# Seven block products in place of eight in one turn of each of seven groups of 1024 columns of the second block's input projection

## The chip, the cores and the metric

The kernel runs on one core of a Trainium2 chip. The metric is the device time of one execution in microseconds (us), the median of the runs. Engines are named as in the profile: PE is TensorE (matmuls), DVE is VectorE, ACT is ScalarE, POOL is GpSimd, SP is SyncE, which issues most DMAs.

## The reference, cut to what matters

```python
# first block, kind 0: gated MLP over 256 tokens, D_MODEL 2048, D_INNER 4096
h = rmsnorm(x, a_norm); z = h @ w_in; ...; x = x + (y * silu(gate)) @ w_out; x = rmsnorm(x, final_norm)
# second block
h = rmsnorm_2(x, norm1_g)
z = h @ w_in                                  # 2048 x 10256
fq, fk = rmsnorm_2 over each head of z        # 8 heads of 128
fv = z[..., 2048:3072]
a_out = forgetting_attention(fq, fk, fv, log_sigmoid(z_f + bias))
mq, mk, mv, m_o = z[..., 4 heads of 128, 128, 256, 256]
m_out = rmsnorm_2(mlstm_chunkwise(mq, mk, mv, i, log_f)) * sigmoid(m_o)
merged = sigmoid(g_a) * (a_out @ w_proj_a) + sigmoid(g_m) * (m_out @ w_proj_m)
x = x + merged @ w_out
h2 = rmsnorm_2(x, norm2_g); u = causal_dwconv(h2 @ w_up); x = x + (silu(u_gate) * u_val) @ w_down
```

All of it is float32, for 256 tokens.

## The kernel before

**Tiling.** Weights stream from HBM in chunks of 256 rows by 512 columns (128 x 1024 in SBUF, 512 KB). SP loads them into a ring of four (`RING`). Every chunk is split in two: ACT rounds it to `w_hi` (L1101), DVE subtracts that from the chunk and gives `w_lo` (L1551). A product in full precision is then three matmuls of 512 columns, hi by hi, hi by lo and lo by hi. A chunk costs PE 12 matmuls: 2 row blocks, 2 token halves, 3 each.

**Order.** All engines walk one list, `ITEMS`. `split(phase, k)` on ACT and on DVE works four items ahead: it waits until PE has done item k, whose ring place comes free, and makes `w_hi` and `w_lo` of item k+4. The steps of ACT and DVE that belong to slot `c` of a phase stand in program order behind that split. PE waits for `lo_ready` before each item.

**Seven products.** In some phases a group has 1024 columns (four PSUM banks of `g`), and in some of its turns of four chunks the 2 x 2 block product is made with seven block products (Strassen-Winograd) of 6 matmuls each in place of four chunks of 12. That takes sums of activations (`sums_of_rows`, `sums_high`, `sums_low`), sums of weight blocks, and sums of the products 1, 5, 6 and 7, which stand in banks of `xs` of their own. In phases `v`, `out1`, `gm0`, `gm1`, `out2` and `down` DVE makes four sums of weight blocks for each such turn (`block_sums`, L1556). In phase `ug` one turn of each of eight groups is made so, with one block sum on DVE and three by adding transfers that POOL issues (`add_block`, L2228). There DVE adds the own products in four instructions (L1751 to L1757) and the halves of the result in two (L1764, L1770).

**Phases around the change.** `vv` (values, 32 chunks, four groups of 512 columns) and `side` (96 chunks: four groups q and k of the attention heads, q and k of the m heads, two groups of output gates, four of gates a) run as plain chunks on PE line L633. Each group has one of two halves of `g`, and ACT takes it out of PSUM. `side` is followed by `gm0`, whose first item is a product; its sums of activations are made by DVE in `side` at slots 88 and 91 (`SUMS_AT` -8, -5; L1641 to L1647), its blocks at the splits of slots 92 on.

Each of the first four groups of `side` passes through `z`: ACT copies it out (slot 8n+7), ACT squares it (slot 8n+8), DVE reduces and makes the mean square (slot 8n+9, L1945 to L1950), POOL makes the power -1/2 (L2213), DVE makes the factor and scales `z` (slot 8n+10, L1956 and L1959), PE turns `z` (`qk_turned`, L681, slots 13, 21, 29, 37), ACT copies to `qk`. The 12 heads start at slot 22 and take four slots each: at step 0 PE makes the scores of head n and the values of head n-1 and DVE the row maximum, at step 1 ACT makes the exponential and DVE the probabilities, at step 3 PE turns them.

## Time and profile before

| | us |
|---|---|
| median of 3 runs | 2088.88 |
| lowest, highest | 2088.44, 2089.41 |
| the profiled execution | 2088.49 |
| its span | 2086.6 |
| PE busy in it | 2079.8 |
| DVE busy | 1575.4 |
| ACT busy | 1142.5 |
| POOL busy | 37.6 |

Busy time is a share of the whole span and says nothing of a stage. `vv` runs from 704 to 794 us and `side` from there to 1098 us. PE's busy time counts each matmul from issue to end, some 390 ns, while the next one starts about 227 ns after it; a short gap of PE doesn't show as idle, and distances of starts tell more.

### The profile page before, as it was taken

The numbers are of one execution on the slowest core, as the hardware profiler recorded it, in microseconds if no ns is written. First come the engines' busy times: TensorE is split into PE (matmuls) and PEld (weight loads), VectorE is DVE, ScalarE is ACT, GpSimd is POOL, SyncE is SP. The second block draws the span as 40 slices with busy tenths as digits, with TensorE's granted clock in tenths as the row PEclk, the third lists the DMA queues.
The fourth block names the chain that finished last, engine by engine and source line by source line (L and its number), as shares of the span: only waits on it lengthen the run. The fifth ranks groups of instructions, "written<-read, shape, count | busy, mean of one in ns | idle before, by whom it ended". The sixth has DMA issues, their size and how long they took to land.

```text
span 2086.6 us, 25362 instructions
## 1 busy us (share of the span) xinstructions
PE 2079.8 (100%) x9952; PEld 1741.3 (83%) x9952; DVE 1575.4 (75%) x1774; ACT 1142.5 (55%) x1354; POOL 37.6 (2%) x41
## 2 busy tenths in 40 slices
PE   9999999999999999999999999999999999999999
PEld 8888888888888887888888888888888888888887
DVE  7988888887888654655669668867777777779986
ACT  6766555555556544554455455555555555555553
POOL 0000000000000000000000000000000000000000
PEclk9999999999999999999999999999999999999999
DMA  9667777778764655544464656455565565556763
GB/s 338 211 197 216 227 235 220 214 245 237 260 229 142 208 192 168 168 159 162 150 219 167 220 172 217 156 188 186 182 194 190 182 199 185 181 183 234 224 206 132
DMA packets 115559, 417.00 MB, mean 200 GB/s; under 512 B 12912, under 2 KB 13680, under 8 KB 114800
## 3 DMA queue, kind: packets, MB, share of 16 engines
q1 hardware_dynamic: 109440, 394.66, 56.4%
q0 software_dynamic: 3456, 12.58, 3.4%
q10 hardware_dynamic: 2544, 8.14, 1.2%
q8 instruction: 79, 1.29, 0.3%
q14 instruction: 40, 0.33, 0.0%
HBM read 413.23 MB, written 2.10 MB: 199 GB/s over the span
## 4 chain that ended last, share of the span: by engine, by line
PE 94%; DVE 3%; DMA 1%; ACT 1%; issue 1%; ACTq 0%; DVEq 0%
PE g L736 34%; PE g L633 21%; PE xs L658 8%; PE g L658 8%; PE xs L759 7%; PE g L763 5%; PE xs L662 4%; PE g L662 4%; DVE w_lo L1551 1%; PE xs L681 1%; DMA gz_block<-in_stream 1%; ACT w_hi L1101 1%; PE xs L918 0%; PE xs L798 0%; DMA raw<-in_stream 0%
## 5 line engine op out<-in xcount | busy, mean ns | idle before, releaser
L1551 DVE TENSOR_TENSOR w_lo<-raw,w_hi 128x1024 fp32r<-128x1024 f32 x643 | 783.0, 1223 | 394.8 <-ACT w_hi L1101 386.9
L1101 ACT ACTIVATE w_hi<-raw 128x1024 fp32r<-128x1024 f32 x643 | 679.6, 1058 | 615.4 <-PE g L633 222.3
L736 PE MATMUL g<-w_hi,in_both 128*128 128x512 f32 x1120 | 356.7, 390 | 1.3 <-DVE w_lo L1622 0.4
L633 PE MATMUL g<-w_hi,mid_both 128*128 128x512 f32 x1024 | 326.6, 394 | 0.0
L736 PEld LDWEIGHTS g<-w_hi,in_both 128*128 128x128 f32 x1120 | 210.2, 188 | 47.0 <-issue 1.8
L633 PEld LDWEIGHTS g<-w_hi,mid_both 128*128 128x128 f32 x1024 | 192.3, 188 | 39.6
L736 PE MATMUL g<-w_lo,in_both 128*128 128x512 f32 x560 | 217.9, 389 | 0.0
L633 PE MATMUL g<-w_lo,mid_both 128*128 128x512 f32 x512 | 199.4, 389 | 0.0
L658 PE MATMUL g<-mlp_both,w_hi 128*128 128x512 f32 x704 | 176.8, 393 | 0.0
L658 PE MATMUL xs<-mlp_both,w_hi 128*128 128x512 f32 x704 | 176.3, 392 | 0.0
L658 PEld LDWEIGHTS g<-mlp_both,w_hi 128*128 128x128 f32 x704 | 126.5, 189 | 22.8
L658 PEld LDWEIGHTS xs<-mlp_both,w_hi 128*128 128x128 f32 x704 | 126.6, 189 | 22.6
L736 PEld LDWEIGHTS g<-w_lo,in_both 128*128 128x128 f32 x560 | 105.1, 188 | 21.3
L633 PEld LDWEIGHTS g<-w_lo,mid_both 128*128 128x128 f32 x512 | 96.3, 188 | 19.1
L662 PEld LDWEIGHTS g<-mlp_both,w_lo 128*128 128x128 f32 x704 | 96.2, 190 | 7.0
L662 PEld LDWEIGHTS xs<-mlp_both,w_lo 128*128 128x128 f32 x704 | 96.1, 190 | 6.8
L662 PE MATMUL g<-mlp_both,w_lo 128*128 128x256 f32 x704 | 98.3, 282 | 0.0
L662 PE MATMUL xs<-mlp_both,w_lo 128*128 128x256 f32 x704 | 98.2, 282 | 0.0
L736 PE MATMUL g<-w_hi,f_hi 128*128 128x512 f32 x240 | 93.6, 390 | 0.1
L736 PE MATMUL g<-w_lo,f_hi 128*128 128x512 f32 x240 | 93.4, 389 | 0.0
L736 PE MATMUL g<-w_hi,f_lo 128*128 128x512 f32 x240 | 93.4, 389 | 0.0
L1101 ACT ACTIVATE w_hi<-d_block 128x1024 fp32r<-128x1024 f32 x49 | 52.0, 1062 | 56.8 <-PE g L736 39.1
(440 smaller groups left out, 3182.6 us busy)
## 6 DMA issues: line engine op xcount, KB each, us to landing
raw<-in_stream SPq DMA_DIRECT2D x643, 512.0 KB, 3.8
d_block<-in_stream SPq DMA_DIRECT2D x28, 512.0 KB, 4.6
o_block<-in_stream SPq DMA_DIRECT2D x24, 512.0 KB, 4.4
v_block<-in_stream SPq DMA_DIRECT2D x20, 512.0 KB, 3.9
ge_block<-in_stream POOLq DMA_DIRECT2D x15, 512.0 KB, 5.5
gm_block<-in_stream SPq DMA_DIRECT2D x12, 512.0 KB, 4.9
ge_block<-in_stream SPq DMA_DIRECT2D x10, 512.0 KB, 4.7
gl_block<-in_stream POOLq DMA_DIRECT2D x6, 512.0 KB, 6.2
```

The lines of the kernel that those rows point to most:

```text
L633: ins = mm(G[buf][:, t, :], a[:, kt, at_t], w[:, slot, j * COLS:(j + 1) * COLS], start=(kt == 0 and n == 0), stop=(last and j == ROWS_PER_ ...
L658: mm(UP[buf][:, b, :, :], w_hi[:, slot, j * COLS + b * P:j * COLS + (b + 1) * P], a_both[:, :, kt, :], start=(kt == 0), stop=False, skip_g ...
L662: ins = mm(UP[buf][:, b, 0, :], w_lo[:, slot, j * COLS + b * P:j * COLS + (b + 1) * P], a_both[:, 0, kt, :], start=False, stop=(last and j ...
L681: ins = turn(TR[:, b, t * P:(t + 1) * P], of[:, t, b * P:(b + 1) * P], ident[:])
L736: ins = mm(GG[:, bank, :], a[:, kt, t * P:(t + 1) * P], w[:, slot, half_chunk(j)], start=n == 0 and opens(item, bank), stop=ended and n == ...
L759: ins = mm(XS[:, own[p], :], a, w[:, slot, half_chunk(j)], start=first and opens_own(item), stop=last and j == 1 and n == 2, skip_group_ch ...
L763: ins = mm(GG[:, RESULT_OF[p], :], a, w[:, slot, half_chunk(j)], start=first and opens(item, RESULT_OF[p]), stop=False, skip_group_check=True)
L1101: activation(w_hi[:, n % RING, :], of[:], ACT.Copy).then_inc(hi_ready, 1)
L1551: v.tensor_tensor(w_lo[:, n % RING, :], of, w_hi[:, n % RING, :].bitcast(F32), ALU.subtract).then_inc(lo_ready, 1)
```

## The change

Phases `vv` and `side` become wide phases: groups of 1024 columns, two in `vv` and six in `side`. In all but the fourth group of `side` turn 0 is made by seven products, in the manner of `ug`. Such a group has 19 items in place of 16 chunks. Three of the 19 (places 5, 10 and 14) have no slot, so that the slots `c` and the steps that go by them stay 16 to a group. ACT copies products 1, 5 and 7 out of their banks; DVE adds them from SBUF, then adds each half of the result in SBUF (`half`). ACT no longer takes these groups from PSUM. The q and k tiles are squared at slots 14, 16, 30 and 32, and turned three slots later; the m heads' q and k at 47 and 49. The mean square and the scaling stay one and two slots behind the squares. The sums of activations for turn 0 are made at the seventh last item of `out1`. POOL's powers are moved to the places of its queue where their inputs come.

```diff
--- before.py
+++ after.py
@@ -67,9 +67,9 @@
 HEAD_AT = 22
 ALL_HEADS = HEADS + M_HEADS
-QK_T_AT = (13, 21, 29, 37, 43, 51)
+QK_T_AT = (17, 19, 33, 35, 47, 49)
+Q_SQUARES_AT = (14, 16, 30, 32)
 QK_TILE = (0, 8, 4, 12, 16, 20)
-VV_OUT = (10, 15, 23, 31)
...
+SUM_TURNS = {"v": (3, 2), "out1": (4, 5), "vv": (0,), "down": (0, 1, 2, 6), "gm0": (3, 2), "out2": (1,)}
+SUMS_AT = {"v": (4, 8), "out1": (2, 6), "vv": (-7,), "down": (3, 6, 9, 64), "gm0": (-8, -5), "out2": (-7,)}
...
-WIDE = tuple(WIDE_STEPS) + ("ug",)
...
+MID_TURN = 0
+MID_PAIRED = ((1, "C0"), (1, "C1"), (1, "C2"), (1, "C3"), (2, "C0"), 1, 5, (2, "C1"), (2, "C2"), (2, "C3"), 7, 6,
+              (3, "C0"), (3, "C1"), 3, 2, 4, (3, "C2"), (3, "C3"))
+MID_SINGLE = ((1, "C0"), (1, "C1"), (1, "C2"), (1, "C3"), (2, "C0"), 1, (2, "C1"), 5, (2, "C2"), (2, "C3"), 7,
+              (3, "C0"), 6, (3, "C1"), 3, 2, 4, (3, "C2"), (3, "C3"))
+MID_PLAIN = tuple((_t, f"C{2 * _h + _k}") for _h in range(2) for _t in range(4) for _k in range(2))
+MID_ORDER = {"vv": (MID_PAIRED,) * 2,
+             "side": (MID_PAIRED, MID_SINGLE, MID_SINGLE, MID_PLAIN, MID_SINGLE, MID_SINGLE)}
+MID_HALF_ENDS = (16, 18)
+NO_SLOT = (5, 10, 14)
+SLOTS = {}
+for _name, _orders in MID_ORDER.items():
+    SLOTS[_name] = []
+    for _g, _order in enumerate(_orders):
+        _c = 16 * _g
+        for _k in range(len(_order)):
+            if len(_order) > 16 and _k in NO_SLOT:
+                SLOTS[_name].append(None)
+            else:
+                SLOTS[_name].append(_c)
+                _c += 1
+SPREAD = ("ug", "vv", "side")
+WIDE = tuple(WIDE_STEPS) + SPREAD
...
+TWO_BANKS = {1: 0, 5: 1, 7: 0, 6: 1}
+ONE_BANK = {1: 1, 5: 1, 7: 1, 6: 1}
...
+BLOCKS_AT = {FIRST_ITEM["vv"] - 5: ("vv", B11), FIRST_ITEM["vv"] - 4: ("vv", B12),
+             FIRST_ITEM["side"] - 3: ("side", B12), FIRST_ITEM["side"] - 2: ("side", B11),
+             FIRST_ITEM["side"] + 66: ("side", B11, 4), FIRST_ITEM["side"] + 67: ("side", B12, 4),
+             FIRST_ITEM["side"] + 88: ("side", B11, 5), FIRST_ITEM["side"] + 89: ("side", B12, 5),
...
+            def opens_mid(item):
+                phase, g, p = item.phase, item.group, item.product
+                ahead, copied, bank = own_ahead(phase, g), 2 * mid_quads(phase, g), own_banks(phase, g)
+                if p == 1:
+                    pe.wait_ge(sem["own_read"], ahead)
+                    if phase == "side" and g in (1, 2):
+                        pe.wait_ge(sem["qk_ready"], 2 * g)
+                    if phase == "side" and g == 4:
+                        pe.wait_ge(sem["scores_read"], ALL_HEADS)
+                if p in (7, 6) and (phase, g) == ("vv", 0):
+                    pe.wait_ge(sem["g_lo_ready"], 4)
+                before = [k for k in (1, 5, 7, 6) if bank[k] == bank[p]]
+                before = before[before.index(p) - 1] if before.index(p) else None
+                if before == 1:
+                    pe.wait_ge(sem["p1_ready"], ahead + 1)
+                if before == 5:
+                    pe.wait_ge(sem["own_copied"], copied + 1)
+                if before == 7:
+                    pe.wait_ge(sem["own_copied"], copied + 2)
...
+            for n in range(items_of("vv")):
+                c = SLOTS["vv"][n]
+                at_item = FIRST_ITEM["vv"] + n
+                item = ITEMS[at_item]
+                pe.wait_ge(lo_ready, at_item + 1)
+                if not item.product and item.group == 0:
+                    pe.wait_ge(sem["g_lo_ready"], item.turn + 1)
+                if item.product == 5 and item.group == 0:
+                    pe.wait_ge(sem["sums_lo_ready"], sums_ahead("vv") + 1)
+                step = wide_product if item.product else wide_chunk
+                step(item, norm_mid.hi, norm_mid.lo, at_item % RING).then_inc(mm_done, 1)
...
                 if n < 4:
                     pe.wait_ge(sem["q_scaled"], n + 1)
                 else:
-                    buf, _, read = group_of("side", n)
-                    pe.wait_ge(group_read[buf], read)
+                    pe.wait_ge(sem["m_scaled"], n - 3)
+                pe.wait_ge(sem["own_read"], own_ahead("side", n // 2 + 1))
                 if n:
                     pe.wait_ge(sem["qk_ready"], n)
                 if heads_before(QK_T_AT[n] + 1):
                     pe.wait_ge(sem["scores_read"], heads_before(QK_T_AT[n] + 1))
-                blocks_turned(z).then_inc(sem["qk_turned"], 1)
+                blocks_turned(wide("side", n // 2).half[n % 2]).then_inc(sem["qk_turned"], 1)
...
-            for c in range(96):
-                one("side", c // 8, c % 8, tokens("side", c // 8, norm_mid.hi, norm_mid.lo))
+            for n in range(items_of("side")):
+                c = SLOTS["side"][n]
+                at_item = FIRST_ITEM["side"] + n
+                item = ITEMS[at_item]
+                pe.wait_ge(lo_ready, at_item + 1)
+                step = wide_product if item.product else wide_chunk
+                step(item, norm_mid.hi, norm_mid.lo, at_item % RING).then_inc(mm_done, 1)
+                if c is None:
+                    continue
...
+            def mid_copies(at_item):
...
+                item = ITEMS[at_item]
+                phase, g, p = item.phase, item.group, item.product
+                if p not in (1, 5, 7):
+                    return
+                if p in (1, 5) and (phase, g) in (("vv", 1), ("side", 0)):
+                    act.wait_ge(sem["vv_out"], (1 if p == 1 else 2) + (2 if phase == "side" else 0))
+                if p == 1 and (phase, g) == ("side", 5):
+                    act.wait_ge(sem["m_values_read"], M_HEADS)
+                act.wait_ge(mm_done, at_item + 1)
+                to = {1: wide(phase, g).p1, 5: wide(phase, g).p5, 7: wide(phase, g).p7}[p]
+                activation(to, XS[:, own_banks(phase, g)[p], :], ACT.Copy).then_inc(sem["p1_ready" if p == 1 else "own_copied"], 1)
+            def half_result(phase, n):
+                buf, _, read = group_of(phase, n)
+                act.wait_ge(group_read[buf], read)
+                return wide(phase, n // 2).half[n % 2]
...
+            def vv_out(n):
+                if n == 0:
+                    act.wait_ge(sem["scale_ready"], 2)
+                by_token(vv[:, :, col_block(n)], half_result("vv", n), ACT.Copy, scale).then_inc(sem["vv_out"], 1)
+            def gate_a_tanh(n):
+                by_token(ga[:, GA_PLACE[n - 8]], half_result("side", n), ACT.Tanh, scale_half).then_inc(sem["ga_ready"], 1)
...
-            for c in range(96):
-                split("side", c)
+                if c in (14, 16, 30):
+                    vv_out((14, 16, 30).index(c))
+            for n in range(items_of("side")):
+                c = SLOTS["side"][n]
+                split("side", n)
+                mid_copies(FIRST_ITEM["side"] + n)
+                if c is None:
+                    continue
                 sums_high("gm0", c - 96)
+                if c == 0:
+                    vv_out(3)
...
-                if c % 8 == 7:
+                if c in (55, 63):
                     n = c // 8
                     product, read, _ = done("side", n)
...
-                if c % 8 == 0 and 8 <= c <= 32:
-                    n = c // 8 - 1
-                    buf, _, read = group_of("side", n)
-                    act.wait_ge(group_read[buf], read)
+                    by_token(mo[:, :, col_block(n - 6)], product, ACT.Tanh, scale_half).then_inc(read, 1)
+                if c in (46, 48):
+                    half = half_result("side", c // 2 - 19)
+                    by_token(half, half, ACT.Copy, scale).then_inc(sem["m_scaled"], 1)
+                if c in (78, 80, 94):
+                    gate_a_tanh({78: 8, 80: 9, 94: 10}[c])
+                if c in Q_SQUARES_AT:
+                    n = Q_SQUARES_AT.index(c)
                     if n:
                         act.wait_ge(sem["q_ms_ready"], n)
-                    activation(z_sq[:], z[:], ACT.Square).then_inc(sem["z_sq_ready"], 1)
+                    activation(z_sq[:], half_result("side", n)[:], ACT.Square).then_inc(sem["z_sq_ready"], 1)
...
+                sums_low("vv", n - items_of("out1"))
+                sums_of_rows("vv", n - items_of("out1"), norm_mid.hi, norm_mid.lo)
...
+            def mid_own_products(phase, n):
...
+                for name, g in GROUPS_BY_PRODUCTS:
+                    if name != phase:
+                        continue
+                    of, at_6 = wide(phase, g), product_item(phase, g, MID_TURN, 6)
+                    after = n - at_6
+                    if after == 0:
+                        dve.wait_ge(sem["p1_ready"], own_ahead(phase, g) + 1)
+                        dve.wait_ge(mm_done, at_6 + 1)
+                        link(v.tensor_tensor(of.u_a, of.p1, XS[:, own_banks(phase, g)[6], :], ALU.subtract))
+                    if after == 1:
+                        dve.wait_ge(sem["own_copied"], 2 * mid_quads(phase, g) + 2)
+                        link(v.tensor_tensor(of.p7, of.p7, of.u_a, ALU.add))
+                    if after == 2:
+                        link(v.tensor_tensor(of.u_a, of.p5, of.u_a, ALU.add))
+                    if after == 3:
+                        v.tensor_tensor(of.p5, of.p5, of.p7, ALU.add).then_inc(sem["own_read"], 1)
...
+            def mid_results(phase, n):
+                for name, g in GROUPS_BY_PRODUCTS:
+                    for h in range(2):
+                        if name == phase and n == half_end(phase, g, h):
+                            buf, end, _ = group_of(phase, 2 * g + h)
+                            half = wide(phase, g).half[h]
+                            dve.wait_ge(mm_done, end)
+                            dve.wait_ge(sem["own_read"], own_ahead(phase, g) + 1)
+                            v.tensor_tensor(half[:], G[h], half[:], ALU.subtract if h else ALU.add).then_inc(group_read[h], 1)
...
-            for c in range(96):
-                split("side", c)
+            for n in range(items_of("side")):
+                c = SLOTS["side"][n]
+                mid_results("side", FIRST_ITEM["side"] + n)
+                split("side", n)
+                mid_own_products("side", FIRST_ITEM["side"] + n)
+                if c is None:
+                    continue
...
-                if c % 8 == 1 and 9 <= c <= 33:
-                    n = c // 8 - 1
+                if c - 1 in Q_SQUARES_AT:
+                    n = Q_SQUARES_AT.index(c - 1)
...
-                if c % 8 == 2 and 10 <= c <= 34:
-                    n = c // 8 - 1
+                if c - 2 in Q_SQUARES_AT:
+                    n = Q_SQUARES_AT.index(c - 2)
                     dve.wait_ge(sem["q_rstd_ready"], n + 1)
+                    if n:
+                        dve.wait_ge(sem["q_scaled"], n)
...
-                    by_head = z[:].rearrange("p t (h d) -> p (t h) d", d=P)
+                    by_head = wide("side", n // 2).half[n % 2][:].rearrange("p t (h d) -> p (t h) d", d=P)
...
                 item = ITEMS[n]
-                if item.phase != "ug" or item.product not in (1, 5, 6):
+                if item.phase not in SPREAD or item.product not in (1, 5, 6):
                     return
-                q, g = quad_of(item), item.group
+                q = quad_of(item)
                 product, to, b = {1: (7, B12, B22), 5: (6, B11, B22), 6: (4, B11, B21)}[item.product]
                 if item.product == 1:
                     pool.wait_ge(sem["block_sums"], sums_made(q, 5))
                 else:
                     pool.wait_ge(lo_ready, n + 1)
-                p.dma_start(wide("ug", g).blocks[to][:], stream[block_row(q, b)], accum_op=ALU.add).then_inc(
+                p.dma_start(wide(item.phase, item.group).blocks[to][:], stream[block_row(q, b)], accum_op=ALU.add).then_inc(
                     sem[f"block_added{product}"], 16)
...
-                if n == FIRST_ITEM["vv"]:
+                if n == FIRST_ITEM["vv"] + 13:
                     rstd(n_rstd[:, 0:2], n_ms[:, 0:2], "ms_ready", 2, "rstd_ready")
                     rstd(n_rstd[:, 2:4], n_ms[:, 2:4], "ms_ready", 3, "rstd_ready")
-                if n == FIRST_ITEM["side"]:
-                    for k in range(4):
+                for k in range(4):
+                    if n == item_at_slot("side", Q_SQUARES_AT[k] + 1) + RING:
                         rstd(q_rstd[:], q_ms[:], "q_ms_ready", k + 1, "q_rstd_ready")
-                    for m in range(M_HEADS):
+                for m in range(M_HEADS):
+                    if n == item_at_slot("side", HEAD_AT + 4 * (HEADS + 1 + m)) + RING:
                         rstd(m_rstd[:], m_ms[:], "m_ms_ready", m + 1, "m_rstd_ready")
```

## Rows read from the trace of the kernel before

**Rows 1.** The page, part 1: busy time of each engine.
```profile
PE 2079.8 (100%) x9952; PEld 1741.3 (83%) x9952; DVE 1575.4 (75%) x1774; ACT 1142.5 (55%) x1354; POOL 37.6 (2%) x41
```
**Rows 2.** Stretches `ug`, `vv`, `side` and start of `gm0`: busy us (instructions), clock, DMA.
```profile
core 0: us, PE busy (x) PEld busy (x) DVE busy (x) ACT busy (x) POOL busy (x), PEclk, DMA share, GB/s
200.00:500.00 300.00, 300.00 (x1353) 248.98 (x1352) 243.94 (x237) 169.07 (x188) 16.12 (x19) 1.00 0.75 229
704.00:794.00 90.00, 90.00 (x407) 74.70 (x406) 48.31 (x53) 45.89 (x63) 1.41 (x2) 1.00 0.59 192
794.00:1098.00 304.00, 303.64 (x1395) 245.99 (x1394) 177.11 (x325) 155.38 (x221) 12.05 (x8) 1.00 0.51 170
1098.00:1113.00 15.00, 15.00 (x68) 12.42 (x67) 14.62 (x13) 9.54 (x10) 0.00 (x0) 1.00 0.53 178
```
**Rows 3.** Timeline of PE: start, length, engine, line: a chunk, product 5 and product 7 begin.
```profile
1099.88 0.39 PE L736 MATMUL g<-w_hi,mid_both 128*128 128x512 f32 x1
...
1102.60 0.39 PE L759 MATMUL xs<-w_hi,gm_sums_hi 128*128 128x512 f32 x1
...
1103.96 0.39 PE L759 MATMUL xs<-w_hi,gm_sums_hi 128*128 128x512 f32 x1
```
**Rows 4.** Timeline of all engines, slots 9 to 13 of `side`: one q tile.
```profile
828.43 1.23 DVE L1551 TENSOR_TENSOR w_lo<-raw,w_hi 128x1024 fp32r<-128x1024 f32 x1 [1.53 <-ACT w_hi L1101]
...
829.58 1.21 DVE L1945 TENSOR_REDUCE q_ss<-z_sq 128x8 f32<-128x1024 f32 x1
...
831.47 2.54 POOL L2213 TENSOR_TENSOR q_rstd<-q_ms,minus_half 128x8 f32<-128x8 f32 x1 [97.16 <-DVE q_ms L1950]
...
834.44 1.22 DVE L1959 TENSOR_TENSOR z<-z,q_factor 128x1024 f32<-128x1024 f32 x1
...
837.97 1.03 PE L681 MATMUL xs<-ident,z 128*128 128x128 f32 x8
838.22 1.06 ACT L1101 ACTIVATE w_hi<-raw 128x1024 fp32r<-128x1024 f32 x1 [1.66 <-PE g L633]
838.76 0.48 PE L633 MATMUL g<-w_hi,mid_both 128*128 128x512 f32 x1
```
**Rows 5.** Timeline of POOL: the power of the fourth q tile.
```profile
905.27 1.64 POOL L2213 TENSOR_TENSOR q_rstd<-q_ms,minus_half 128x8 f32<-128x8 f32 x1 [24.07 <-DVE q_ms L1950]
```
**Rows 6.** Timeline of PE at step 0 of a head: scores and values.
```profile
876.82 0.44 PE L915 MATMUL xs<-head_row,ones_r 64*128 64x384 f32 x1
...
878.38 0.39 PE L943 MATMUL xs<-probs_t,vv 128*128 128x128 f32 x2
```
**Rows 7.** Timeline of DVE: last slots of `side`, first items of `gm0`.
```profile
1088.99 1.23 DVE L1551 TENSOR_TENSOR w_lo<-raw,w_hi 128x1024 fp32r<-128x1024 f32 x1 [1.50 <-ACT w_hi L1101]
1090.14 1.22 DVE L1596 TENSOR_TENSOR gm_sums_lo<-gm_sums,gm_sums_hi 128x1024 fp32r<-128x1024 f32 x1
1091.27 1.22 DVE L1641 TENSOR_TENSOR gm_rows<-mid_both 128x1024 f32<-128x1024 f32 x1
...
1094.12 1.22 DVE L1551 TENSOR_TENSOR w_lo<-gm_block,w_hi 128x1024 fp32r<-128x1024 f32 x1
1095.47 1.23 DVE L1556 TENSOR_TENSOR gm_block<-gm_block,gm_block 128x1024 f32<-128x1024 f32 x1
...
1102.42 1.22 DVE L1551 TENSOR_TENSOR w_lo<-gm_block,w_hi 128x1024 fp32r<-128x1024 f32 x1
```
**Rows 8.** Timeline of DVE in `ug`: an own-product sum and the instruction behind it, a half's result.
```profile
257.66 0.68 DVE L1755 TENSOR_TENSOR ge_gate<-xs,ge_gate 128x512 f32<-128x512 f32 x1
258.38 1.23 DVE L1551 TENSOR_TENSOR w_lo<-raw,w_hi 128x1024 fp32r<-128x1024 f32 x1
...
261.26 1.22 DVE L1764 TENSOR_TENSOR ge_act<-g,ge_act 128x1024 f32<-128x1024 f32 x1
```
**Rows 9.** What reads or writes `ge_block` in `ug`: issue, and time to landing of its DMAs.
```profile
L2228 POOL DMA_DIRECT2D ge_block<-in_stream x15: 865/865/1056, 179.2 to 378.9; - x15
...
DMA to landing us min/median/max: 4.2/5.4/7.5
```

127 lines of the change are left out of this document (83 added, 44 removed).

## Prediction

> **What bounds the kernel now.** I read the page's busy times first [rows 1]: PE has work in flight in all but 7 us of the span, DVE in 75%, ACT in 55%. That is a mean, so the table by stage comes next [rows 2]: in `vv` PE is in flight 90.00 us of 90 and in `side` 303.64 of 304, at granted clock 1.00 (2.4 GHz), while DVE has 48 and 177 us of work. The stage behind them is another matter: from 1098 to 1113 DVE works 14.62 us of 15. Then the distances of starts: a chunk of 12 matmuls takes 2.72 us, from 1099.88 to 1102.60, and a product of six takes 1.36, from there to 1103.96 [rows 3]. So 0.227 us a matmul is the price on the path in both stages, and whatever makes PE wait for DVE is added to it.
>
> Last the time that a step needs, counted from the end of a PE item, E. PE turns the first q tile at 837.97 [rows 4]; four chunks earlier, at 827.09, slot 9 ended. DVE's `w_lo` starts 1.34 after E (828.43), and its next instruction at 829.58.
>
> **What is taken away.** Seven groups (two in `vv`, five in `side`) each make eight blocks as seven: 48 matmuls become 42. 7 x 6 x 0.2267 = 9.5 us less on PE, all of it on the path.
>
> **What is added, beside other work.** For each group: three more items to split (DVE 3 x 1.14, ACT 3 x 1.06), one block sum (1.15), four own-product sums of 0.72 and two results of 1.14 [rows 7, 8], 9.7 us of DVE in 40. The stage's DVE share goes from 54% and 58% to about 78% and 76%. `ug` carries the same scheme with 243.94 of 300 us of DVE and 0.75 of the DMAs, and PE is in flight in all of it [rows 2]. So the means leave room, and the scheme alone I cost at nothing: PE and the ring of four cover it. ACT's three copies of products (0.6 each, an estimate at half of a full 1.06 tile) have cover in both stages at 51% ACT. The three added DMAs of a group land in 4.2 to 7.5 us [rows 9]; product 4 in the order with lone products is the tightest. Its block can be asked for 2.6 us after place 8 ends, lands 0.9 + 5.4 later and needs 2.3 for the split, 11.2 in all, where PE comes to it after 13.6: nothing, and nothing up to a landing of 7.8. The moved sums at the end of `out1` put 4 us of DVE on one item of 2.72 and plain chunks follow: 0 to 1 us, taken as 0, since the items behind have 1.6 us each to spare. In POOL's queue each power now stands behind the adding transfers whose inputs come before it, and a transfer takes POOL 0.87 us [rows 9], ahead of the power's start: nothing. The removed ACT copies out of PSUM were off the path: nothing.
>
> **What comes onto the path, first place: the q and k tiles.** Before, a tile's mean square is made at slot 9, scaled at 10, turned at 13: PE has four chunks, 10.9 us, between the end of slot 9 and the turn, and DVE finishes at 834.44 + 1.22 = 835.66, 8.6 after it [rows 4]. So 2.3 us are spare. After, the mean square is made at slot 15, scaled at 16, and turned at 17: two chunks, 5.4 us. The chain doesn't get shorter. From the start of the reduction to the end of the scaling it takes 835.66 - 829.58 = 6.08 us, of which POOL's power is 2.54 [rows 4].
> - First tile. At slot 15 DVE first adds the second half (starts at E + 0.3, 1.14), then splits (1.14): the reduction starts at E + 2.6, the scaling ends at E + 8.7, PE is there at E + 5.4. Wait 3.2.
> - Second tile, turned at slot 19. Its reduction stands on DVE behind the first scaling, a split and the block sum for product 1: 1.14 + 1.25 + 6.08 = 8.5 after that scaling. PE has the first turn (0.9, rows 4 from 837.97 to 838.76) and slots 18 and 19: 6.4. Wait 2.1.
> - Third tile, turned at 33, as the first, with a head's step 0 and 1 on DVE ahead of it and in POOL's shadow: 3.3.
> - Fourth tile, at 35: PE has two steps more, a turn of probabilities and the scores and values at slot 34, 1.95 us [rows 6], which nearly cover it: 0 to 0.5, taken as 0.3.
>
> Together 8.9 us. If POOL's power takes 1.64 us, as once [rows 5], the four come to about 5.9. I take 8.9, since the other rows of that instruction are 2.54. Behind these waits are PE's next items, whose splits are done by then, so they cost nothing more and give nothing back.
>
> **Second place: the seam of `side` and `gm0`.** Before, DVE makes the second sums of activations (1091.27 to 1094.12) and then, without a pause, the splits and block sums of `gm0`; the split of its product 7 ends at 1102.42 + 1.22 = 1103.64 [rows 7] and PE wants it at 1103.96 [rows 3]. Only 0.3 us are spare. After, the sums stay at slots 88 and 91, now places 9 and 13 of a group of 19 items whose tail has product 6, then 3, 2 and 4, and DVE's own-product sums. Take time 0 at PE's end of place 12. Place 13 ends at 2.72 and DVE starts its split 1.34 later, at 4.06. In order it then has, up to the split of `gm0`'s product 7: three splits (3.4), three splits with block sums (7.2, like 1094.12 to 1096.62 three times less the waits), two `sums_low` (2.26), the sums of activations (2.85), three own-product sums (2.16) and two results (2.28). That is 20.1 and ends at 24.2. PE's items until then are 3 chunks (places 13, 17, 18), 3 products, and `gm0`'s product 1, chunk, product 5: 4 x 2.72 + 5 x 1.36 = 17.7. Wait 6.5 in all, seen in parts: at place 18 (its split is behind the sums), at product 1 of `gm0` (own bank not yet read), at its first chunk and at product 7. It can be 5.5 if a link wait or two falls away. It can be 7.4 if the block of product 4 lands at the slow end of 7.5 [rows 9]. Behind product 7, DVE catches up within three items. I add nothing.
>
> **Sum.** 2088.49 - 9.5 + 8.9 + 6.5 = 2094.4 for an execution like the profiled one. That one lay 0.39 under the median of 2088.88, so the forecast in medians is 2094.8. A measurement of this kernel can tell about 0.2% (4.2 us) from no change, so the bounds are 2084.7 and 2093.1.
>
> **Rivals.**
> - *The change works as in `ug`, with no waits.* For it: the same scheme in rows 2, at more DVE load. Against it: `ug` has no POOL step ahead of a turn two slots later and no sums of activations in its tails. Time 2088.9 - 9.5 = 2079.4. This is the other side, and one mechanism decides it: whether DVE is ahead of PE at the two places. It needs the q chain under 5.4 us from the end of slot 15, where rows 4 has 8.6. Chance 0.08.
> - *Only one place is real.* PE's waits at the tiles give the ring time, or the seam's DVE work is overlapped more than in my order: -9.5 + 8.9 gives 2088.3, -9.5 + 6.5 gives 2085.9. Chance 0.15, time 2088.
> - *The product tails under heads are too dense.* In groups 1, 2 and 4 of `side` DVE has a head's steps beside own-product sums; probabilities of the head of place 12 are ready some 0.2 us before PE turns them after place 16. If that chain is 1 us longer, three groups give 3 us: 2097.8. Chance 0.12.
> - *The clock falls in the waits.* In the trace PE never waits 3 us and its clock is 1.00 in each stretch [rows 2], so no row shows what follows a wait of 3.2. At 1.2 GHz a chunk would take 2.72 us more at most; one after each of two long waits gives 2094.8 + 5.4 = 2100.2. Chance 0.08. The Trainium skill (TensorE: Matmul & The Clock Gate, "HAM oscillation") says that PE's clock is halved after idle time in the middle of a kernel. By that rule the long waits would be followed by slow matmuls; no run here shows it yet.
>
> **How the numbers follow.** The forecast has 0.57, with its own range 2090.8 (short powers and the lean seam, 5.9 + 5.5) to 2096.5. Range: 2086.0 takes in most of the one-place case and leaves the no-wait case out; 2100.0 takes in dense tails and most of the clock's. Slower by over 0.2%: all of the dense and clock cases, and four fifths of the forecast's, 0.66. Faster: the no-wait case and a little of the seam-only one, 0.10. The same: 0.24.
>
> **What would show it.** Right: PE's start distances in `vv` stay at 0.227 us with 42 matmuls fewer in both stages; PE waits of 2 to 3.5 us just before the turns of q and k, at three of four, with POOL's power ending 1.6 us before each; DVE without a pause from slot 91 to `gm0`'s product 7, and PE waiting for `w_lo` and `own_read` there. Wrong: a turn with no wait, DVE idle at the seam, or a wait in `vv` or at product 4. The prediction fails most likely by the size of the tile waits, which rest on POOL's 2.54.

## The result, and the profile after

The changed kernel takes 2100.45 us (median, 2098.47 to 2101.49), the kernel before beside it 2088.74: 1.0055 times as long, 95% interval 1.0037 to 1.0072. The direction was as forecast, the time 5.7 us above the forecast and 0.45 above the range. Measured again later on another occasion it took 2098.69. The profiled execution took 2100.55 us, its span is 2098.8.

The page's busy time of PE (time, share of the span, instructions) has the 42 matmuls fewer, and yet PE works less of the span:

```profile
PE 2076.6 (99%) x9910; PEld 1735.3 (83%) x9910; DVE 1644.8 (78%) x1850; ACT 1171.6 (56%) x1393; POOL 55.5 (3%) x62
```

By stage (busy time and instructions per engine, granted clock of PE, DMA share), against [rows 2]:

```profile
core 0: us, PE busy (x) PEld busy (x) DVE busy (x) ACT busy (x) POOL busy (x), PEclk, DMA share, GB/s
704.00:795.00 91.00, 91.00 (x411) 75.53 (x410) 69.08 (x75) 56.31 (x77) 7.69 (x8) 1.00 0.78 234
...
845.00:870.00 25.00, 18.91 (x82) 15.10 (x80) 14.84 (x23) 10.02 (x10) 6.06 (x4) 0.86 0.52 135
870.00:1098.00 228.00, 225.61 (x1036) 182.43 (x1036) 166.19 (x297) 130.46 (x196) 15.07 (x16) 1.00 0.62 187
1098.00:1111.00 13.00, 9.77 (x41) 7.14 (x40) 12.59 (x16) 7.35 (x8) 0.00 (x0) 1.00 0.57 213
1111.00:1122.00 11.00, 8.47 (x31) 6.51 (x30) 9.61 (x9) 5.63 (x7) 0.00 (x0) 0.84 0.44 146
```

In `vv` PE is in flight all the time at full clock, as before. It is missing 6.1 us from 845 to 870, 2.4 from there to 1098, 3.2 from 1098 to 1111 and 2.5 behind that. In two of the stretches the granted clock is 0.86 and 0.84, where each stretch before had 1.00. What PE waited for from 795 to 1120 (total, times, the longest):

```profile
engine line waited for: us in total, times, longest us
PE xs L781 <- DVE mq_half L2177: 6.1, 2, 4.8
PE xs L884 <- DVE w_lo L1725: 2.5, 1, 2.5
PE xs L781 <- DVE mk_half L2177: 2.4, 1, 2.4
...
PE xs L1017 <- DVE gl L2137: 0.8, 1, 0.8
```

These are the two places of the prediction: line 781 turns a q or k tile and waits for the scaling, and the rest of the large ones belong to the seam. Line 1017, the running sums of the gates, was in no step.

**The tiles.** All engines around the first two turns (start, length, engine, line, operation; in brackets the idle time before it and its releaser):

```profile
844.97 1.21 DVE L2161 TENSOR_REDUCE q_ss<-z_sq 128x8 f32<-128x1024 f32 x1
...
845.94 0.39 PE L861 MATMUL g<-w_hi,mid_both 128*128 128x512 f32 x1
...
846.70 1.22 DVE L1725 TENSOR_TENSOR w_lo<-raw,w_hi 128x1024 fp32r<-128x1024 f32 x1
...
846.87 2.57 POOL L2431 TENSOR_TENSOR q_rstd<-q_ms,minus_half 128x8 f32<-128x8 f32 x1 [27.82 <-DVE q_ms L2166]
...
851.15 1.97 PE L781 MATMUL xs<-ident,mq_half 128*128 128x128 f32 x8 [4.83 <-DVE mq_half L2177]
...
852.77 0.78 PE L861 MATMUL g<-w_hi,mid_both 128*128 128x512 f32 x1
...
853.77 1.05 PE L861 MATMUL g<-w_hi,mid_both 128*128 128x512 f32 x2
...
855.41 1.66 POOL L2431 TENSOR_TENSOR q_rstd<-q_ms,minus_half 128x8 f32<-128x8 f32 x1 [0.62 <-DVE q_ms L2166]
...
855.79 0.62 PE L861 MATMUL g<-w_hi,mid_both 128*128 128x512 f32 x2
...
858.06 1.23 DVE L1725 TENSOR_TENSOR w_lo<-raw,w_hi 128x1024 fp32r<-128x1024 f32 x1 [2.74 <-ACT w_hi L1243]
...
859.21 0.39 PE L861 MATMUL g<-w_hi,mid_both 128*128 128x512 f32 x1
...
860.87 0.86 PEld L781 LDWEIGHTS xs<-ident,mq_half 128*128 128x128 f32 x8 [1.69 <-DVE mq_half L2177]
```

The last matmul before the first turn begins at 845.94, the turn at 851.15, 5.21 later where a matmul takes 0.227: 4.99 us of waiting. Before the second turn it is 860.87 - 859.21 - 0.23 = 1.43. The chunk at 852.77 starts at half clock: it has a matmul of 0.78 and at 853.77 two in 1.05; at 855.79 two take 0.62 again. The granted clock was 0.5 for 6.8 us, from 848.3, still within the wait, to 855.1. The third tile:

```profile
903.57 1.66 POOL L2431 TENSOR_TENSOR q_rstd<-q_ms,minus_half 128x8 f32<-128x8 f32 x1 [25.86 <-DVE q_ms L2166]
...
904.16 0.39 PE L861 MATMUL g<-w_hi,mid_both 128*128 128x512 f32 x1
...
906.94 0.86 PEld L781 LDWEIGHTS xs<-ident,mk_half 128*128 128x128 f32 x8 [2.81 <-DVE mk_half L2177]
```

906.94 - 904.16 - 0.23 = 2.55. The fourth turn has no wait. POOL's power took 2.57 us for the first tile and 1.66 for the others. The first starts 0.17 us behind the start of a split on DVE (846.70); the second, at 855.41, starts with no split running, DVE's next being at 858.06.

**The seam.** PE around product 7 of `gm0`, and what DVE has in that time:

```profile
1111.34 0.39 PE L884 MATMUL xs<-w_hi,gm_sums_lo 128*128 128x512 f32 x1
1114.27 0.60 PE L884 MATMUL xs<-w_hi,gm_sums_hi 128*128 128x512 f32 x1 [2.53 <-DVE w_lo L1725]
1114.66 0.63 PE L884 MATMUL xs<-w_lo,gm_sums_hi 128*128 128x512 f32 x1
```

```profile
1111.86 1.22 DVE L2083 TENSOR_TENSOR mb_half<-g,mb_half 128x1024 f32<-128x1024 f32 x1
1113.00 1.22 DVE L1725 TENSOR_TENSOR w_lo<-gm_block,w_hi 128x1024 fp32r<-128x1024 f32 x1
```

DVE goes from instruction to instruction and ends the split at 1114.22; PE starts product 7 at 1114.27 and had been free since 1111.57: 2.70 us. Then come matmuls of 0.63 in place of 0.39, for 3.4 us at granted clock 0.5. The same difference of starts gives 1.75 at place 18, 1.06 at product 1 and 0.91 at the first chunk of `gm0`: 6.42 with product 7.

### The profile page after: what moved, and what is told of

The parts are those of the page before. It is cut to its first block, busy times and chain, and to the rows that moved or that the text cites. A ratio compares the mean times of both kernels' runs of the same rounds, so it can differ in the third digit from the quotient of the medians.

```text
span 2098.8 us, 25523 instructions
## 1 busy us (share of the span) xinstructions
PE 2076.6 (99%) x9910; PEld 1735.3 (83%) x9910; DVE 1644.8 (78%) x1850; ACT 1171.6 (56%) x1393; POOL 55.5 (3%) x62
## 4 chain that ended last, share of the span: by engine, by line
PE 89%; DVE 6%; DMA 2%; ACT 2%; issue 1%; POOL 0%; ACTq 0%; DVEq 0%
PE g L861 44%; PE xs L884 9%; PE xs L758 8%; PE g L758 8%; PE g L888 5%; PE g L733 4%; PE xs L762 4%; PE g L762 4%; DVE w_lo L1725 2%; ACT w_hi L1243 1%; PE xs L781 1%; DMA raw<-in_stream 1%; DMA gz_block<-in_stream 1%; PE xs L923 0%; PE xs L1053 0%
## 5 line engine op out<-in xcount | busy, mean ns | idle before, releaser
L1725 DVE TENSOR_TENSOR w_lo<-raw,w_hi 128x1024 fp32r<-128x1024 f32 x629 | 765.2, 1223 | 312.2 <-ACT w_hi L1243 303.4
L1243 ACT ACTIVATE w_hi<-raw 128x1024 fp32r<-128x1024 f32 x629 | 664.4, 1058 | 550.4 <-PE g L861 233.8
L861 PE MATMUL g<-w_hi,mid_both 128*128 128x512 f32 x960 | 312.8, 395 | 2.3 <-DVE w_lo L1725 2.3
L861 PEld LDWEIGHTS g<-w_hi,mid_both 128*128 128x128 f32 x960 | 181.3, 189 | 40.7 <-DVE w_lo L1725 3.2
L861 PE MATMUL g<-w_lo,mid_both 128*128 128x512 f32 x480 | 187.7, 391 | 0.0
L861 PEld LDWEIGHTS g<-w_lo,mid_both 128*128 128x128 f32 x480 | 90.7, 189 | 18.1
```

The source lines that it names most:

```text
L861: ins = mm(GG[:, bank, :], a[:, kt, t * P:(t + 1) * P], w[:, slot, half_chunk(j)], start=n == 0 and opens(item, bank), stop=ended and n == ...
L1243: activation(w_hi[:, n % RING, :], of[:], ACT.Copy).then_inc(hi_ready, 1)
L1725: v.tensor_tensor(w_lo[:, n % RING, :], of, w_hi[:, n % RING, :].bitcast(F32), ALU.subtract).then_inc(lo_ready, 1)
```

## The experiments

"Waits" below are distances of starts less the 0.227 of a matmul, as above. Every time is the median beside that of the kernel before on the same chip, which was 2088.87 to 2088.99 in all of them. Only one execution of a kernel has a trace. Of the others the record has the time, the span and the mean granted clock; a stretch of 3.4 us at half clock lowers that mean by 0.0008, from 1.000 to 0.999. It was 1.000 in all but one of 68 executions of the kernel before, and 0.997 to 0.998 in the four of the changed kernel.

### Which places hold the loss

**no_scaling** takes the chain out of the q and k tiles (squares on ACT, mean square and scaling on DVE, power on POOL) and leaves the turns where they are. The result lacks the norm of q and k.

```diff
-                    pe.wait_ge(sem["q_scaled"], n + 1)
+                    buf, _, read = group_of("side", n)
+                    pe.wait_ge(group_read[buf], read)
...
-                if c in Q_SQUARES_AT:
...
-                if c - 1 in Q_SQUARES_AT:
...
-                if c - 2 in Q_SQUARES_AT:
...
-                        rstd(q_rstd[:], q_ms[:], "q_ms_ready", k + 1, "q_rstd_ready")
```


> The changed kernel with the norm of q and k left out (squares, mean square, power and scaling; the tiles are turned as soon as the halves are added), so a part of the computation is missing. Theory A (PE waits at the turns because the chain of DVE, POOL and DVE from the mean square to the scaling is longer than the two chunks that PE has): all waits at the turns vanish, 9.0 us, and the 6.8 us at half clock behind the first of them too, worth about 2; time 2100.45 - 11 = 2089.5, with the four waits at the seam to gm0 unchanged at 6.4 us. Theory B (PE waits in these stages because DVE as a whole is too full in a group of 19 items): half or less of the waits goes, since the DVE work left out is only 13 us, and waits appear elsewhere; 2095 or more.

2089.54 (1.0002, interval 0.9993 to 1.0012). In the trace no wait at a turn is left, and no stretch at half clock; the waits of the seam are the same to 0.02 us (1.75, 1.06, 0.91, 2.72). From the first matmul of `vv` to the first of `pa0`, the phase behind `gm0`, this trace has 434.1 us, the changed kernel's 447.1 and the one before 435.4. So the tile waits (9.0) and the two stretches at half clock (3.7, below) make up nearly all of the 12.9 between the two. The stretch at the seam was absent here with the seam's waits in place, which is the first sign that a wait doesn't always bring it. The traced execution is not the usual one in this: the mean clock was 1.000 in three of the ten and 0.999 in seven, which took 1.4 us more on average. Where their stretch lies no trace shows; the seam has the only waits over 2 us.

**last_plain** makes the last side group in sixteen plain chunks.

```diff
-             "side": (MID_PAIRED, MID_SINGLE, MID_SINGLE, MID_PLAIN, MID_SINGLE, MID_SINGLE)}
+             "side": (MID_PAIRED, MID_SINGLE, MID_SINGLE, MID_PLAIN, MID_SINGLE, MID_PLAIN)}
...
```


> The changed kernel with the last group of side made of 16 plain chunks again. Theory A (the seam waits are DVE work that piles up behind the sums of activations for gm0, because the group's tail has short items and six more DVE instructions): the four waits of 6.4 us go, and with them the 3.4 us at half clock, worth 1.7; one product is lost, 1.4. Time 2100.45 - 6.4 - 1.7 + 1.4 = 2093.7. Theory B (the seam waits come from late blocks of gm0, DMA traffic having risen): the waits stay at 3 us or more and the time is 2098 or more.

2093.85 (1.0023, 1.0014 to 1.0033). By stretches, at the tiles and at the seam:

```profile
845.00:870.00 25.00, 20.65 (x99) 16.37 (x98) 16.59 (x27) 11.68 (x12) 6.07 (x4) 1.00 0.61 157
...
1098.00:1111.00 13.00, 13.00 (x58) 10.47 (x57) 12.86 (x12) 8.49 (x9) 0.00 (x0) 1.00 0.37 122
```

The seam is whole again, PE 13.00 of 13 and DVE 12.86. The tiles still cost 3.23, 1.44 and 2.56, at full clock in this execution, which took 2090.85. The ten times spread from 2090.7 to 2097.8, more than those of any other kernel here, and the clock on record goes with them: 1.000 in the two fastest, 0.999 in four of 2092.4 to 2094.6, 0.998 in four of 2093.9 to 2097.8. So the slower ones had stretches at half clock, and the median of 2093.85 holds some clock that the trace lacks. It met the expectation of 2093.7, which had counted the 5.0 of the first tile, in part by luck.

**both_away** joins the two edits. Apart from them only the gates remain.

> The changed kernel with its last side group plain and without the scaling of q and k by their norm (mean squares, powers and scaling are left out; the turns stand at 17, 19, 33 and 35 as in the change). Theory A (the two places and the gates are all that the change adds to the path): 6 groups by products save 6 x 1.36 = 8.2 us, the gates take 1.0: 2088.9 - 8.2 + 1.0 = 2081.7. Rival (part of the saving is lost to something that the two places hide, such as product 4's block): 2084 or more.

2083.21 (0.9971, 0.9960 to 0.9983), 1.5 above the expectation. From `vv` to `pa0`, as above, this trace has 428.56 us, the one before 435.37: 6.8 less, where 8.2 - 1.0 = 7.2 were counted. So 0.4 us of small waits are unaccounted for in these stages. The rest of the 1.5 lies outside the span: the median of the seven spans is 2080.3, of those before 2087.1, 6.8 less as well, while a time is 2.1 to 3.4 us over its span here and mostly 1.8 before. All seven had clock 1.000. The block of product 4 and the other covered terms took no more than the 0.4.

### Whether the waits come from where the turns stand

**before_early_turns** is the kernel before, without a product in `side`, with the turns two slots earlier.

```diff
-QK_T_AT = (13, 21, 29, 37, 43, 51)
+QK_T_AT = (11, 19, 27, 35, 43, 51)
```


> The kernel before the change, with the turns of q and k at slots 11, 19, 27 and 35 in place of 13, 21, 29 and 37: two chunks between the mean square's slot and the turn, as in the change, with no product anywhere. Theory A: the chain takes 8.6 us from the end of slots 9, 17, 25 and 33 and PE has 5.4, so each turn waits 2.3 (power 1.66) to 3.2 us (power 2.56): 2088.9 + 9 to 13 = 2098 to 2102, no fall of the clock if waits of 3.2 are short enough for it, and 1.7 us more for each stretch of 3.4 us at half clock if not. Rival (the waits come from the product tails and not from where the turns stand): 2089 to 2091.

2103.76 (1.0071, 1.0055 to 1.0086), more than the expectation without the clock, and inside it with the clock. All engines at the first turn:

```profile
833.51 0.39 PE L633 MATMUL g<-w_hi,mid_both 128*128 128x512 f32 x1
...
836.94 1.57 PEld L681 LDWEIGHTS xs<-ident,z 128*128 128x128 f32 x8 [3.46 <-DVE z L1959]
...
838.56 0.78 PE L633 MATMUL g<-w_hi,mid_both 128*128 128x512 f32 x1
```

The wait is 836.94 - 833.51 - 0.23 = 3.20, as the chain of [rows 4] gives it (8.6 less 5.4). The others are 3.20, 2.19 and 0.65, sum 9.2. So the waits belong to two chunks between mean square and turn; no product is needed for them. And each of the three waits over 2 us lowers the clock, for 3.4 us each time:

```profile
826.00:840.00 14.00, 10.96 (x47) 8.97 (x46) 9.29 (x16) 5.87 (x7) 2.54 (x1) 0.89 0.52 167
```

(the columns as in the first such table). The second and the third turn have 0.91, from 860 to 880 and from 880 to 900. Without the clock the sum was 2088.9 + 9.2 = 2098.1; 5.6 more were measured. In the trace 5.0 of them lie between the first matmul of `vv` and the first of `pa0` (449.6 us, 435.4 before, less the 9.2).

### What the clock costs

**filled_waits** has small matmuls of ones ahead of the first turn and of product 7.

```diff
+                if c == 17:
+                    for _ in range(8):
+                        mm(PT[:, 0:P], ones[:], ones[:], start=True, stop=True)
...
+                    if p == 0 and n == 3:
+                        for _ in range(5):
+                            mm(PT[:, 0:P], ones[:], ones[:], start=True, stop=True)
```


> The changed kernel with eight added matmuls of 128 columns of ones (about 3.4 us) ahead of the turn of the first q tile and five (2.1 us) ahead of product 7 of gm0, both in places where PE waits anyway and into a bank that is written afresh. Theory A (the waits also cost clock: 10.2 us at 0.5 in the changed kernel, of which 7.4 with work, so 3.7 us): the waits keep their places, the granted clock stays at 1.00, and the time falls by 3 to 3.7, to 2097. Theory B (the clock's fall costs nothing that the waits don't): no change, 2100.5, or more by what the added matmuls overrun.

2096.28 (1.0036, 1.0022 to 1.0049): 4.2 us faster than the change, 2.4 than its second measurement. The clock is 1.00 throughout in the traced execution; of the five, two had 0.999 and took 1.8 us more on average. Here the first tile waits 3.2 in all, 1.8 of them under the fillers, and not 5.0, so the gain isn't the clock's alone. Its trace compares better with after_again, below, which has the same waits at the tiles and the seam: from `vv` to `pa0` 441.8 us here and 445.0 there, 3.2 for two stretches at half clock.

**early_filled** does the same to the kernel with early turns, with 24, 24 and 16 fillers.

> The kernel before with early turns (slots 11, 19, 27, 35), and 24, 24 and 16 small matmuls of ones ahead of the first three turns, which are shorter than the waits there, so that PE works while it waits. Theory A (the clock fell because PE stood still, and the three stretches of 3.4 us at half clock cost 1.7 us each): the waits of 3.2, 3.2 and 2.2 stay, the stretches go: 2103.8 - 5.1 = 2098.7. Rival (the stretches come from the turn itself or from the power drawn, not from standing still): 2103 to 2104.

2104.61: no gain, although the clock stayed at 1.00. The expectation had the length of a filler wrong: the trace has two instructions of 0.11 us for each, 5.35 us ahead of the first turn where the wait is 3.20. The run shows that PE at work keeps the clock up, and nothing of the price.

**early_short_fill** has 13, 13 and 9 of them, shorter than the waits.

```diff
-                    for _ in range((24, 24, 16)[QK_T_AT.index(c)]):
+                    for _ in range((13, 13, 9)[QK_T_AT.index(c)]):
```


> As early_filled, with 13, 13 and 9 small matmuls of ones instead of 24, 24 and 16. In that run the trace shows two instructions of 0.11 us for each of them (48 in 5.35 us ahead of the first turn), so that they took 5.35, 5.35 and 3.57 us in place of waits of 3.20, 3.20 and 2.19: the clock stayed full, but the time didn't fall. Thirteen take 2.9 us and nine 2.0, inside the waits. Theory A (standing still lowers the clock, and a stretch of 3.4 us at half clock costs 1.7 us): the ends of the waits stay where they are, the three stretches go: 2103.8 - 5.1 = 2098.7. Rival (the stretches go but something else takes their time): 2103 or more.

2098.34 (1.0048, 1.0031 to 1.0065). PE at the first turn, and the same stretch of time:

```profile
832.73 0.40 PE L633 MATMUL g<-w_hi,mid_both 128*128 128x512 f32 x1
832.97 3.06 PE L973 MATMUL xs<-ones 128*128 128x128 f32 x26
836.16 1.09 PE L681 MATMUL xs<-ident,z 128*128 128x128 f32 x8
```

```profile
826.00:840.00 14.00, 13.87 (x79) 11.96 (x78) 8.97 (x16) 5.16 (x5) 2.54 (x1) 1.00 0.50 172
```

836.16 - 832.73 - 0.23 = 3.20: the wait is the same, and filled. Against before_early_turns 5.4 us are gone by the medians, 1.8 for each stretch of 3.4 us at half clock. Of the 5.5 by which the two spans differ 0.8 lie ahead of `vv`, where the kernels are the same; from `vv` to `pa0` it is 449.6 and 444.9, so 1.6 for each stretch. What is left over 2088.9 is 9.4, the waits themselves. One of the four executions had clock 0.999 and took 2100.72, so fillers don't rule the fall out.

**after_again** is the changed kernel once more, to see what of its trace recurs.

> The changed kernel as it is, once more beside the others. Theory A: 2098.5 to 2101.5 as before; in its profile waits at the turns of tiles 1 to 3 and at the seam as before, tile 1 between 3.2 us (ring load in time) and 5.0; one or two stretches at half clock. Rival (the wait of 5.0 and both stretches were of that one execution): median under 2097.

2098.69 (1.0047, 1.0034 to 1.0061). Its first tile, and the clock of the two stretches:

```profile
838.15 1.07 ACT L1243 ACTIVATE w_hi<-raw 128x1024 fp32r<-128x1024 f32 x1 [1.87 <-DMA raw<-in_stream]
...
842.89 1.21 DVE L2161 TENSOR_REDUCE q_ss<-z_sq 128x8 f32<-128x1024 f32 x1
...
845.61 0.39 PE L861 MATMUL g<-w_hi,mid_both 128*128 128x512 f32 x1
...
849.07 1.65 PE L781 MATMUL xs<-ident,mq_half 128*128 128x128 f32 x8 [3.07 <-DVE mq_half L2177]
```

```profile
845.00:870.00 25.00, 20.65 (x91) 16.43 (x90) 15.02 (x19) 11.42 (x12) 5.85 (x4) 0.93 0.56 139
...
1110.00:1120.00 10.00, 8.08 (x28) 6.50 (x29) 8.63 (x8) 5.99 (x7) 0.00 (x0) 0.83 0.55 164
```

The waits are 3.23, 1.44 and 2.54 at the tiles and 6.42 at the seam, and both stretches at half clock recur. Its four executions have 0.999, 0.998 twice and 0.997. What doesn't recur is the 5.0: in the first trace ACT had been waiting for a ring load at the tail of group 0,

```profile
840.47 1.06 ACT L1243 ACTIVATE w_hi<-raw 128x1024 fp32r<-128x1024 f32 x1 [3.86 <-DMA raw<-in_stream]
```

3.86 us, here 1.87 (at 838.15). With it DVE's reduction started at 844.97, here at 842.89; 0.3 of the 2.1 is a shift of the whole trace. That the load is late because three products in a row use up the ring in half the time is my reading; no run isolates it.

### Where products can go without the waits

**five_groups** makes products in `vv` and in groups 0, 2 and 4 of `side`, and turns at 19, 21, 29 and 36.

```diff
-QK_T_AT = (17, 19, 33, 35, 47, 49)
-Q_SQUARES_AT = (14, 16, 30, 32)
+QK_T_AT = (19, 21, 29, 36, 47, 49)
+Q_SQUARES_AT = (14, 16, 24, 32)
-             "side": (MID_PAIRED, MID_SINGLE, MID_SINGLE, MID_PLAIN, MID_SINGLE, MID_SINGLE)}
+             "side": (MID_PAIRED, MID_PLAIN, MID_SINGLE, MID_PLAIN, MID_SINGLE, MID_PLAIN)}
...
```


> The changed kernel with groups 1 and 5 of side plain, so products in two groups of vv and in groups 0, 2 and 4 of side; q and k tiles squared at slots 14, 16, 24 and 32 and turned at 19, 21, 29 and 36, the tiles of the plain group through a buffer of their own. Theory A (a group made by products costs PE nothing by itself; only the early turns and the sums at the seam cost): five times 1.36 = 6.8 us less than before, 1 us more at the gate logits as in the changed kernel, no wait over 1 us at a turn or the seam, clock 1.00: 2088.7 - 5.8 = 2082.9. Theory B (each such group costs PE something of its own, in heads above all): 2086 to 2090.

2087.70 (0.9992, 0.9983 to 1.0002), 4.8 above Theory A. No turn waits. But the fourth turn is now right ahead of product 1 of group 2, which writes the bank that ACT first has to copy out (PE, then ACT):

```profile
908.94 1.06 PE L786 MATMUL xs<-ident,z 128*128 128x128 f32 x8
912.10 0.47 PE L889 MATMUL xs<-w_hi,mid_both 128*128 128x512 f32 x1 [2.10 <-ACT qk L1574]
```

```profile
910.86 1.10 ACT L1574 ACTIVATE qk<-xs,par 128x1024 f32<-128x1024 f32 x1
```

The wait moved behind the turn: 2.27 us, and 3.4 us at half clock behind it. With 1.6 to 1.8 for that stretch and 1.0 at the gates that makes 4.9 to 5.1. Five of the ten executions had 0.999 and five 1.000, with means of 2088.0 and 2086.8.

**held_turns** keeps all seven groups and gives both what seemed to be missing, later turns and product 1 one chunk later.

```diff
-QK_T_AT = (17, 19, 33, 35, 47, 49)
+QK_T_AT = (18, 20, 35, 36, 47, 49)
+MID_HELD = MID_SINGLE[:5] + (MID_SINGLE[6], 1) + MID_SINGLE[7:]
-             "side": (MID_PAIRED, MID_SINGLE, MID_SINGLE, MID_PLAIN, MID_SINGLE, MID_SINGLE)}
+             "side": (MID_PAIRED, MID_HELD, MID_HELD, MID_PLAIN, MID_SINGLE, MID_SINGLE)}
```


> The changed kernel with all its seven groups, but the turns of q and k at slots 18, 20, 35 and 36 and product 1 of groups 1 and 2 of side one chunk later. Theory A: the chain from the end of slot 15 takes 8.7 us and meets PE after 8.2, so tile 1 waits 0.5, tile 2 about 1.3 to 2.2, tiles 3 and 4 nothing; the first stretch at half clock goes too, the seam's 6.4 and its clock stay: 2100.4 - 9.0 + 2.3 - 1.9 = about 2091.9, 2090 if the seam's clock holds. Theory B (the tile chain moves its wait to product 1, which now waits for the copy of the turned tile): 2094 or more.

2096.68 (1.0037, 1.0023 to 1.0050): Theory A missed by 4.8. The tiles wait 0.51 and 0.74, but the fourth 2.61, since its turn now follows the third's by one chunk; and product 5, which stands right behind product 1, waits 1.95 and 1.62. Together 7.4, as much as the 7.2 they replace. The clock stayed full in the traced execution, the fastest (2095.24); the other three had 0.999 and took 2096.6 to 2098.0.

**five_held** has that order of products in group 2 alone, with DVE's `gl` one item sooner.

```diff
-             "side": (MID_PAIRED, MID_PLAIN, MID_SINGLE, MID_PLAIN, MID_SINGLE, MID_PLAIN)}
+             "side": (MID_PAIRED, MID_PLAIN, MID_HELD, MID_PLAIN, MID_SINGLE, MID_PLAIN)}
-                if c == 5:
+                if c == 4:
                     dve.wait_ge(sem["ln_ready"], 1)
```


> Products in vv and in groups 0, 2 and 4 of side, 1, 3 and 5 plain, turns of q and k at slots 19, 21, 29 and 36, as in the run with five groups; but product 1 of group 2 stands one chunk later, behind slot 36 plus one chunk, and DVE takes the logarithms of the gates one item sooner. Theory A (waits as counted, clock a consequence of a wait): the wait of 2.3 us ahead of product 1 at 909.7 goes, since ACT's copy of the turned tile has a chunk of 2.7 us beside it, with it the stretch at half clock behind it (about 1.8 us), and the wait of 1.0 us before the running sums; 2087.7 - 2.3 - 1.8 - 1.0 = 2082.6. Theory B (the fewer matmuls are given back elsewhere, whatever is done to these waits): 2086 to 2088.

2084.29 (0.9978, 0.9970 to 0.9987), 1.7 above Theory A, and the trace has them (PE and ACT):

```profile
912.50 1.06 ACT L1252 ACTIVATE w_hi<-mk_block 128x1024 fp32r<-128x1024 f32 x1 [0.30 <-PE xs L890]
913.46 0.58 ACT L1513 ACTIVATE mk_half<-xs 128x512 f32<-128x512 f32 x1
...
914.19 0.47 PE L890 MATMUL xs<-w_hi,mid_sums_hi 128*128 128x512 f32 x1 [1.46 <-ACT mk_half L1513]
```

Product 5 at 914.19 waits 1.62 us for ACT's copy of product 1, which is queued behind two splits. The wait at the running sums of the gates, 0.99, is gone with the earlier `gl`; the one at the logits, 0.65, stays.

**five_apart** puts a chunk between products 1 and 5.

```diff
-MID_HELD = MID_SINGLE[:5] + (MID_SINGLE[6], 1) + MID_SINGLE[7:]
+MID_HELD = MID_SINGLE[:5] + ((2, "C1"), 1, (2, "C2"), 5) + MID_SINGLE[9:]
```


> As five_held, but with a chunk between products 1 and 5 of group 2, as in the order with lone products. In five_held PE waited 1.62 us at 912.46 ahead of product 5, whose bank ACT had not yet copied out. Theory A (a wait counted is a wait given back): 2084.3 - 1.6 = 2082.7. Rival (the wait moves to product 7 or to a block that lands late): 2084 or more.

2082.84 (0.9972, 0.9961 to 0.9983), faster than both kernels. Its stretches from the tiles over the rest of `side` to the seam:

```profile
795.00:925.00 130.00, 129.47 (x600) 104.12 (x599) 86.44 (x149) 73.43 (x99) 14.52 (x10) 1.00 0.60 176
925.00:1098.00 173.00, 173.00 (x790) 140.54 (x790) 123.08 (x211) 96.54 (x141) 5.54 (x7) 1.00 0.58 186
1098.00:1111.00 13.00, 13.00 (x60) 10.74 (x58) 11.02 (x11) 7.21 (x8) 0.00 (x0) 1.00 0.81 276
```

PE misses 0.5 us in all three together. From `vv` to `pa0` it takes 6.5 us less than before, of the 6.8 that 30 matmuls are worth.

**vv_alone** has products in `vv` only.

> Products in the two groups of vv alone, side plain throughout, turns of q and k as before the change. 12 matmuls fewer at 0.2267 us are 2.7 us. Theory A (the scheme costs nothing in vv but about 0.3 us more at the gate logits and 0.7 at the running sums): 2088.9 - 2.7 + 1.0 = 2087.2 to 2086.2. Theory B (product tails cost waits in vv too): 2089 or more.

2086.19 (0.9988, 0.9979 to 0.9997), the lower end of Theory A: 2.7 us for 12 matmuls, and in sum no more at the gates than before: PE waits 0.64 us at the gate logits and 0.02 at the running sums, 0.32 and 0.31 before. So the 0.99 at the running sums belongs to `side`'s group 0, not to `vv`.

## Why the prediction fell short

- *PE saves 9.5 us.* Right: in `vv`, where nothing waits, the rate is 0.227 a matmul, and vv_alone and five_apart give back 2.7 and 6.5 for 12 and 30 matmuls (2.7 and 6.8 at that rate).
- *The tile waits, 8.9.* The sum was met (4.99 + 1.43 + 2.55 + 0 = 8.97) by luck, since errors of its terms cancel. The first was 1.8 over its 3.2, by the late ring load; after_again has 3.23, the predicted chain. The second and third were 0.7 below, since POOL's power took 1.66 and not 2.54. I named both values [rows 4, 5] and took the long one for all; a short power is what these traces show where no split of DVE is running as it starts, and that is so at tiles 2 to 4. Without the late load the place costs 7.2. What decides it, two chunks for a chain of 8.6, before_early_turns shows without any product.
- *The seam, 6.5.* Right in sum and parts: 6.42, at place 18, product 1, the first chunk and product 7, with DVE going from instruction to instruction (12.59 of the 13 us from 1098). last_plain removes it.
- *The scheme alone at nothing.* Right for `vv`, product 4 and the rest of the tails, but for the gates: PE waits 0.65 and 0.99 there, 0.32 and 0.31 before, 1.0 more. The running sums (PE, then the wait):

```profile
815.09 0.39 PE L861 MATMUL g<-w_hi,mid_both 128*128 128x512 f32 x1
816.30 0.39 PE L1017 MATMUL xs<-gl,late 128*128 128x12 f32 x2 [0.83 <-DVE gl L2137]
```

wait for `gl`, which on DVE stood behind three splits (from 812.54 to 816.06), one of them that of a product's block. I had walked through the queues at the turns and the seam, and not at the gates, which are queued in the same slots.
- *The clock.* This is the step that failed, and the largest part of what took the result over the range. I had it as a rival with a chance of 0.08 that excludes the forecast, and its own time, 2100.2, lay above the bound of 2100.0. It is no alternative to the waits but follows from them: if they came as forecast, it was to be added to the sum, with the chance that a wait of that length lowers the clock. That the trace before showed no such wait was no reason for a small chance. Its price was 5.4 for two stretches; filled_waits and early_short_fill give 1.6 each in the traces, 1.8 by the medians of the latter. In the changed kernel the two stretches cost 3.7, read as the lengthened distances of starts in them (2.0 and 1.8; the first stretch is 6.8 us long, but PE stood still in 2.9 of them). All eight executions of the changed kernel had some of it on record.

Together, from 2088.9: -9.5 + 9.0 + 6.4 + 1.0 + 3.7 gives 2099.5 for the profiled case, and with 7.2 at the tiles and 3.4 for the clock 2097.4 for the usual one; 2100.45 and 2098.69 were measured. From `vv` to `pa0` both traces have 1.1 more than these terms (11.7 and 9.6 us over the kernel before). Of that 0.4 is what both_away has too, with the same products under the heads, so the dense tails of the third rival are no more than that. Another 0.1 goes behind each wait, where the first matmul starts 0.34 us before the next and not 0.23 (behind the seam's at 1101.05 and 1107.34, for instance). The rest I haven't followed.

The Trainium skill (TensorE: Matmul & The Clock Gate, "HAM oscillation"), cited in the prediction, was right that idle time in mid-kernel halves the clock. It names a length of gap to stay under, and here the waits of 2.19 (before_early_turns) and 2.27 us (five_groups), both shorter than it, were followed by 3.4 us at half clock; the measurement decides.

## What to carry to other kernels

A step that saves work on the bound engine shortens the time in which the other engines' chains had to finish. Before it is placed, write down for each wait of that engine how many of its items lie between the start of the chain and the wait, before and after; the profile before has the chain's length already. If a wait of 2 us or more comes out, add the clock to the sum, with its chance: here it fell behind eight of sixteen. And a wait taken away at one point has its successor at the next user of the same bank or engine: of four rearrangements here only the one that gave each of them an item of cover kept the gain, with fewer products and not more.
